# A decoder step with 32 experts: adding the experts' rows to the tokens through DRAM, or on chip with 0/1 matrices

## What is computed

```python
h = h + hier_moe(rmsnorm(h, norm2_g), rg_w, rg_b, re_w, re_b, e_wg, e_wu, e_wd)
...
for gi in range(N_GROUPS):            # 4 groups of 8 experts
    h = silu(einsum('nd,edf->nef', xt, e_wg[gi])) * einsum('nd,edf->nef', xt, e_wu[gi])
    out = out + einsum('nef,efd->nd', h * comb[:, gi, :, None], e_wd[gi])
...
y_prompt, y_sample = rmsnorm(hp, final_g), rmsnorm(hs, final_g)
```

## Time and profile before

| | us |
|---|---|
| median of three runs | 1273.19 (1273.01 to 1273.73) |
| profiled execution | 1273.13 |
| its span | 1271.0 |
| outside its span | 2.1 |

### The profile page before, as it was taken

The page is one execution under the profiler, slowest core; times in us unless marked ns, Lnnn a source line. Parts: engine busy times, 40 slices in busy tenths (PEclk is TensorE's granted clock), DMA queues, the critical chain, the costliest instruction groups (busy, mean ns, idle before and its releaser), DMA issues.

```text
span 1271.0 us, 22247 instructions
## 1 busy us (share of the span) xinstructions
PE 1176.8 (93%) x9742; PEld 851.4 (67%) x9742; DVE 452.2 (36%) x814; ACT 322.7 (25%) x568; POOL 93.1 (7%) x132
## 2 busy tenths in 40 slices
PE   8999899999999999999999998999888887888885
PEld 7889789898898789999998884333333332333331
DVE  5347856553464453333334142121111111111116
ACT  5454333444315452322323231000000000000004
POOL 2100000001000100000000002111111111111100
PEclk9999999999999999999999999999999999999998
DMA  8210103202324822232236488999999999999995
GB/s 244 68 34 2 35 14 82 82 2 72 133 67 127 248 84 76 82 93 75 77 115 223 163 314 318 419 419 417 419 419 420 419 420 419 420 419 419 420 419 215
DMA packets 113419, 283.18 MB, mean 223 GB/s; under 512 B 23779, under 2 KB 71093, under 8 KB 88746
## 3 DMA queue, kind: packets, MB, share of 16 engines
q1 hardware_dynamic: 107546, 269.93, 56.0%
q0 software_dynamic: 5120, 9.46, 2.0%
q10 hardware_dynamic: 656, 2.36, 0.5%
HBM read 273.44 MB, written 15.60 MB: 227 GB/s over the span
## 4 chain that ended last, share of the span: by engine, by line
PE 66%; DMA 19%; DVE 6%; SPq 6%; issue 1%; ACT 1%; DVEq 0%; ACTq 0%
DMA slot<-in_e_wu_dram 18%; PE bank L1465 7%; PE bank L670 7%; PE bank L1398 6%; PE bank L1400 6%; PE bank L1399 6%; SPq L619 6%; PE bank L677 4%; PE bank L1525 2%; PE bank L1526 2%; PE bank L1527 2%; PE bank L1684 1%; PE bank L1638 1%; PE bank L1695 1%; PE bank L1577 1%
## 5 line engine op out<-in xcount | busy, mean ns | idle before, releaser
L670 PE MATMUL bank<-slot,xs 128*64 128x512 f32 x512 | 248.3, 634 | 60.8 <-DMA slot<-in_e_wu_dram 59.9
L671 PE MATMUL bank<-slot,xs 128*64 128x512 f32 x512 | 249.4, 637 | 0.0
L670 PEld LDWEIGHTS bank<-slot,xs 128*64 128x64 f32 x512 | 69.8, 145 | 204.5 <-issue 201.4
L1034 DVE TENSOR_TENSOR xs<-bank,g2x 128x512 f32<-128x512 f32 x32 | 22.1, 691 | 315.6 <-PE bank L803 315.6
L1398 PE MATMUL bank<-xnh,wh 128*128 128x256 f32 (+1 forms) x448 | 133.1, 297 | 0.6 <-DVE mt L3029 0.6
L1400 PE MATMUL bank<-xnh,low 128*128 128x256 f32 (+1 forms) x448 | 132.6, 296 | 0.0
L1399 PE MATMUL bank<-xnl,wh 128*128 128x256 f32 (+1 forms) x448 | 132.6, 296 | 0.0
L905 ACT ACTIVATE sg<-bank 64x512 f32<-64x512 f32 x32 | 19.0, 593 | 444.2 <-PE bank L671 444.2
L2581 DVE TENSOR_TENSOR low<-ring,wh 128x1536 fp32r<-128x1536 f32 (+1 forms) x45 | 89.9, 2005 | 78.2 <-ACT wh L2220 71.1
L677 PE MATMUL bank<-slot,ht 128*64 128x512 f32 x512 | 116.9, 598 | 0.5 <-DVE ht L1062 0.5
L1398 PEld LDWEIGHTS bank<-xnh,wh 128*128 128x128 f32 x448 | 85.0, 190 | 1.3 <-issue 1.2
(11 more groups left out here) (529 smaller groups left out, 2096.5 us busy)
## 6 DMA issues: line engine op xcount, KB each, us to landing
slot<-in_e_wg_dram SPq DMA_DIRECT2D x64, 1024.0 KB, 27.7
slot<-in_e_wu_dram SPq DMA_DIRECT2D x64, 1024.0 KB, 27.8
slot<-in_e_wd_dram SPq DMA_DIRECT2D x64, 1024.0 KB, 28.2
ring<-in_w_in_dram SPq DMA_DIRECT2D x13, 1024.0 KB, 5.4
ring<-in_w_in_dram SPq DMA_DIRECT2D x24, 512.0 KB, 4.3
ring<-in_w_branch_dram SPq DMA_DIRECT2D x24, 256.0 KB, 4.8
kvs<-in_cache_mem_k_dram SPq DMA_DIRECT2D x8, 512.0 KB, 5.7
kvs<-in_cache_mem_v_dram SPq DMA_DIRECT2D x8, 512.0 KB, 5.9
```

The costliest lines, as they stand in the source:

```text
L670: pe.matmul(out[64:128, :], tok, wg[:, FF * k:FF * k + FF], start=(k == 0), stop=(k == KD - 1))
L671: mm = pe.matmul(out[0:64, :], tok, wu[:, FF * k:FF * k + FF], start=(k == 0), stop=(k == KD - 1))
```

## The change

- The scatters, the list of their rows, the clearing of two experts' rows and the reading back are removed. POOL only gathers.
- A token's slot and expert are one number, its code (slot times 32 plus expert). TensorE copies the codes of all tokens to all partitions (`code12` against the identity; ACT to `vsel`). `pcode` holds the code that each partition of a pair's stacked block stands for. DVE's `choose(i)` compares them: `wse[c]`, 128 slots of experts 2i and 2i + 1 by 576 tokens, is 1 where the token chose that slot.
- Routing weights by slot and expert (`cs`) come from 20 further small products. ACT scales an expert's output by them on the way from PSUM (`yh`, rounded for a fast matmul), DVE forms what the rounding left (`yl`). `flip` puts an odd expert's halves the other way round, so that two experts' outputs stack to 128 partitions.
- `mix(i, t)`: four matmuls add the stacked block to token tile t in two PSUM banks (`yh` by two column halves, then `yl`). DVE's `add` brings the sum into `h`. A pair's five tiles stand inside the next odd expert's `gate_up`, one behind each of steps 2 to 6; the last pair's follow the last `down`.
- Gate/up and down have one PSUM bank each instead of two. DVE makes `h2` before `evacuate(e + 1)`, and `yl` before `ht`.
- SP's load of expert 2's third matrix waits for the slot weights (`pe_t` "weights") instead of `wcol`.

The core of the diff (helpers, the overflow loops and tile lists are left out):

```diff
@@ moe_sp
-            dve_t.wait(sp, "weights")
+            pe_t.wait(sp, "weights")
...
-            for n in range(2):
-                sp.wait_ge(scattered[n], 16 * (EX // 2 - 1))
-            sp.wait_ge(cleared, 32)
             general_sp(sp)
-            for t, (t0, tn) in enumerate(TILES):
-                for k in range(2):
-                    sp.dma_start(yb[t][0:tn, D * k:D * k + D], y_d.rearrange("(n k) d -> n k d", k=2)[t0:t0 + tn, k, :])\
-                        .then_inc(yb_loaded[t][k], 16)
@@ moe_pe
-            dve_t.wait(pe, "weights")
+            dve_t.wait(pe, "lists")
             for i in range(2):
                 for t, (_, tn) in enumerate(TILES):
                     to = psum[6 - 2 * i][:, 128 * t:128 * t + tn] if t < 4 else psum[5][:, 64 * i:64 * i + 64]
-                    for p in (0, 64):
-                        mm = pe.matmul(to[p:p + 64, :], wcol[0:tn, 5 * i + t, :], ident[0:tn, 0:tn], start=True, stop=True)
+                    mm = pe.matmul(to, code12[0:tn, i, t:t + 1].to_broadcast([tn, 128]), ident[0:tn, 0:tn], start=True, stop=True)
+            pe_t.done(mm, "codes")
+            idle_products(pe, 7, 8)
+            dve_t.wait(pe, "cw")
+            cw = post[:, :, :, :].rearrange("p k t e -> p (k t) e")
+            for n in range(10):
+                tn = TILES[n % 5][1]
+                for p in (0, 64):
+                    mm = pe.matmul(psum[HT_BANK][p:p + 64, 0:EX], place1[0:tn, n, :], cw[0:tn, n, :], start=(n == 0), stop=(n == 9))
             pe_t.done(mm, "weights")
-            idle_products(pe, 7, 8)
+            def mix(i, t):
+                t0, tn = TILES[t]
+                n = 5 * i + t
+                if t == 0:
+                    dve_e.wait(pe, ("chosen", i))
+                    act_e.wait(pe, ("yh", 2 * i + 1))
+                if n >= 2:
+                    pe.wait_ge(added, n - 1)
+                for y in (yh, yl):
+                    if t == 0 and y is yl:
+                        dve_e.wait(pe, ("yl", 2 * i + 1))
+                    for c in range(2):
+                        mm = pe.matmul(psum[MIX_BANK[n % 2] + c][0:tn, :], wse[c][:, t0:t0 + tn], y[:, c, :],
+                                       start=(y is yh), stop=(y is yl))
+                mm.then_inc(mixed, 1)
             def gate_up(e):
...
+                for k in range(KD):
...
+                    mm = expert_in(pe, psum[0], xs[e % 2], slots[3 * e % NSLOT], slots[(3 * e + 1) % NSLOT], range(k, k + 1))
...
+                    if e >= 3 and e % 2 and 2 <= k <= 6:
+                        mix(e // 2 - 1, k - 2)
             def down(e):
                 dve_e.wait(pe, ("ht", e))
-                if e >= 2:
-                    dve_e.wait(pe, ("y", e - 2))
+                if e >= 1:
+                    dve_e.wait(pe, ("yl", e - 1))
+                    act_e.wait(pe, ("yh", e - 1))
...
+            down(EX - 1)
+            for t in range(5):
+                mix(TWO - 1, t)
             general_pe(pe)
@@ moe_act
+            for e in range(EX + 1):
+                if e < EX:
...
+                    act_e.done(act.activation(sg[:, :], psum[0][64:128, :], ACT.Silu), ("silu", e))
...
+                if e:
+                    pe_m.wait(act, ("d", e - 1))
+                    if e % 2 and e >= 3:
+                        act.wait_ge(mixed, 5 * (e // 2))
+                    for r in range(2):
+                        rows_ = slice(64 * r, 64 * r + 64)
+                        last = act.activation(yh[rows_, r ^ (e - 1) % 2, :], psum[Y_BANK][rows_, :], ACT.Copy, scale=cs[rows_, e - 1:e])
+                    act_e.done(last, ("yh", e - 1))
@@ moe_dve
+            def choose(i):
+                if i >= 1:
+                    dve.wait_ge(mixed, 5 * i)
+                for c in range(2):
+                    last = dve.tensor_scalar(wse[c][:, :], vsel[:, 0, :], pcode[:, c, i:i + 1], None, ALU.is_equal)
+                seq(last)
+                for c in range(2):
+                    last = dve.scalar_tensor_tensor(wse[c][:, :], vsel[:, 1, :], pcode[:, c, i:i + 1], wse[c][:, :], ALU.is_equal, ALU.add)
+                dve_e.done(last, ("chosen", i))
+            def add(i, t):
...
+                dve.wait_ge(mixed, n + 1)
+                hv = h[0:tn, t, :].rearrange("p (c n) -> p c n", c=2)
+                dve.tensor_tensor(hv, hv, banks8[0:tn, bank:bank + 2, :], ALU.add).then_inc(added, 1)
             evacuate(0)
+            act_t.wait(dve, "codes")
             for e in range(EX + 1):
-                if e + 1 < EX:
-                    evacuate(e + 1)
+                if e >= 3 and e % 2:
+                    for t in range(5):
+                        add(e // 2 - 1, t)
...
+                if e + 1 < EX:
+                    evacuate(e + 1)
                 if e:
-                    pe_m.wait(dve, ("d", e - 1))
-                    if e >= 3:
-                        dve.wait_ge(scattered[(e - 1) % 2], 16 * ((e - 1) // 2))
-                    dve_e.done(dve.tensor_copy(yo[(e - 1) % 2][:, :], psum[4 + (e - 1) % 2][:, :]), ("y", e - 1))
+                    act_e.wait(dve, ("yh", e - 1))
+                    for r in range(2):
...
+                        last = dve.scalar_tensor_tensor(yl[rows_, c, :], psum[Y_BANK][rows_, :], cs[rows_, e - 1:e], yh[rows_, c, :],
+                                                        ALU.mult, ALU.subtract)
+                    dve_e.done(last, ("yl", e - 1))
...
+                if e % 2:
+                    choose(e // 2)
...
+            for t in range(5):
+                add(TWO - 1, t)
             general_dve(dve)
...
+            for t in range(5):
+                final(t)
@@ moe_pool
-            gather(0)
-            for e in (EX - 2, EX - 1):
-                pool.indirect_dma_start(y_rows, bass.IndirectOffsetOnAxis(il[:, 1, e:e + 1].bitcast(U32), 0), xg[1][:, :], None,
-                                        bounds_check=4 * NT - 1, oob_is_err=False).then_inc(cleared, 16)
-            pool.wait_ge(cleared, 32)
-            for e in (1, 2):
+            for e in range(EX):
                 gather(e)
-            for e in range(EX - 2):
-                if e + 3 < EX:
-                    gather(e + 3)
-                dve_e.wait(pool, ("y", e))
-                pool.indirect_dma_start(y_rows, bass.IndirectOffsetOnAxis(il[:, 1, e:e + 1].bitcast(U32), 0), yo[e % 2][:, :], None,
-                                        bounds_check=4 * NT - 1, oob_is_err=False).then_inc(scattered[e % 2], 16)
```

More of the change, by code:

```diff
@@ L591, in build @@
         dve_o = Steps(sem("dve_o"), ["wr"] + [x for c in range(OUTS) for x in [("h", c, t) for t in range(5)] + ([("lg", c)] if c < OUTS - 1 else [])])
[L592 to L597, removed]
+        pe_t = Steps(sem("pe_t"), ["pos", "lists", "codes", "weights"])
+        mixed, added = sem("mixed"), sem("added")
+        TWO = EX // 2
+        act_t = Steps(sem("act_t"), ["root"] + [("x2", t) for t in range(5)] + ["exp_g", "exp_e", "codes"])
+        dve_t = Steps(sem("dve_t"), ["clear", "sumsq", "ms", "rstd", "lg", "dg", "sel", "places", "rows", "code", "lists", "addr", "de", "c12", "cw"])
+        dve_l = Steps(sem("dve_l"), ["zeros", "even", "gather0", "scatter0", "gather", "scatter"] + [("more", t, k) for t in range(5) for k in range(2)])
         pool_t = Steps(sem("pool_t"), ["far", "rows", "xg"])
@@ L806, in gate_up @@
             def gate_up(e):
                 dve_e.wait(pe, ("xs", e))
-                if e >= 2:
[L809 to L814, removed]
+                if e >= 1:
+                    dve_e.wait(pe, ("h", e - 1))
@@ L895, in moe_act @@
             act_t.done(act.activation(pg[:, 3, :], pg[:, 3, :], ACT.Exp), "exp_e")
-            pe_t.wait(act, "weights")
+            pe_t.wait(act, "codes")
             for i in range(2):
-                act.activation(wsel[:, i, 0:SEQ], psum[6 - 2 * i][:, :], ACT.Copy)
-            act_t.done(act.activation(wsel[:, :, SEQ:NT], psum[5][:, 0:2 * NS].rearrange("p (i n) -> p i n", i=2), ACT.Copy), "weights")
-            for e in range(EX):
-                pe_m.wait(act, ("gu", e))
-                if e >= 1:
-                    dve_e.wait(act, ("h", e - 1))
-                act_e.done(act.activation(sg[:, :], psum[e % 2][64:128, :], ACT.Silu), ("silu", e))
@@ L1181, in general_act @@
         def general_act(act):
-            dve_e.wait(act, ("h", EX - 1))
             with act.If(some_overflow(act)):
@@ L1212, in general_dve @@
                         dve_n.done(dve.tensor_copy(yg[:, :], psum[4][:, :]), "y")
+                dve.wait_ge(yb_loaded, 16 * 5)
+                for t, (_, tn) in enumerate(TILES):
+                    for k in range(2):
+                        if k:
+                            dve_l.wait(dve, ("more", t, 0))
+                        dve_l.done(dve.scalar_tensor_tensor(h[0:tn, t, :], yb[t][0:tn, D * k:D * k + D], c12[0:tn, k, t:t + 1], h[0:tn, t, :],
```

(4 more changed lines are left out.)

213 lines of the change are left out of this document (88 added, 125 removed).

## The result

The changed kernel took 1277.3 us (median of 20 runs, 1274.5 to 1283.2), the one before 1273.8 us in the same session (20 runs, 1270.7 to 1276.7): a ratio of 1.0032 (95% interval 1.0023 to 1.0040), so slower by a third of a per cent. The profiled execution took 1277.25 us, its span is 1275.5. The time forecast was 1275.1.

The account below looks back on a forecast made before the run. Transfers bound the loop before; TensorE was to become the bound. Loop end at 1242.7 plus 30.3 behind it gives a span of 1273.0, with 2.1 outside 1275.1 us against 1273.13; range 1260 to 1288.

Parts of the forecast that it names:

- The likeliest case: Over the loop: TensorE becomes the bound at the prices of the rows, 1275.1 us, within 1270 to 1280; chance 0.60.
- The switches: Mixed tiles in `gate_up`: 0.91 us streaming plus 0.09, 0.10, 0.09 and 0.05 for array changes, 1.25 a tile, 6.25 a pair.
- The hidden loads of the rival: At the switches in mixed tiles, loads go ahead of the matmuls: a tile costs 1.10 us, 1264 us in all; chance 0.13.
- The loop's end: Last gate and up products at 1242.7 us, 7.8 later than before: 791.64 + 0.3 + 357.0 + 93.8.
- Beside TensorE: ACT's and DVE's scaling and adds (1.25 us each) in the loop hide behind TensorE, which waits for none of them.
- the rival of the late low part: In `gate_up`, mixing waits for `yl`: 1297 us; chance 0.20, shared with other TensorE waits of 0.5 to 1.2 us a pair.
- The end: From the last gate and up products to the span's end: 30.3 us instead of 36.1, so 5.8 us won.
- the double evacuation: Behind each of the last two `down`s: `yh` 1.2 us, then `yl` 1.25 and 1.3; one copy of 0.69 stood there before.
- One sign: Late in the expert loop, the DMA engines' busy share was to fall below 1.

Follow-up runs that it names:

- Fewer stops: The changed kernel with a pair's five tiles mixed at three places of the gate instead of five: 1267.46 us, ratio 0.9944.
- the doubled low part: The changed kernel with the two matmuls of the low part issued twice in every tile: 1315.57 us, ratio 1.0316.
- the kernel with fewer bytes: The changed kernel with the third matrix loaded for experts 0 to 2 only and used for all others: 1277.24 us, ratio 1.0029.
- The kernel that mixes beside the transposes: The changed kernel with tiles two behind step 4, two right ahead of `turn_in`, one right behind it: 1264.35 us, the second time 1265.39 us.
- the last experiment: The kernel mixing beside the transposes, with the last `down` in another PSUM bank and the last `ht` ahead of `yl`: 1259.58 us, ratio 0.9878.

## Why the prediction was right

The likeliest case came true: TensorE became the bound and took back what the lighter transfers allowed. The time came out 2.2 us above the forecast, inside its range. The forecast time, 1.9 us above the kernel before, would have counted as no change; the 3.5 us measured are slower by more than 0.2%, which its range held too.

- **The switches.** A pair cost 6.29 us ((1244.05 - 792.65 - 357.0) / 15) where 6.25 were forecast from rows of other products. Fewer stops (0.33 us for a way in and back) and the doubled low part (0.47 a tile for two matmuls) measure the two shares apart: 0.92 + 0.34 = 1.26, where 1.25 was forecast. The Trainium skill, "TensorEngine Tiling (Array Packing)", section "Key Properties", states that a change of the tiling mode drains TensorE. The trace agrees, with 0.1 us at each change. The other part of the price is a load that isn't hidden. The hidden loads of the rival, 11 us less, are seen at no switch here.
- **The loop's end.** It was forecast for 1242.7 and came at 1244.05: 0.7 from a later start, 0.6 from the pairs. The first `turn_in` came 1.40 us later than before (773.15 against 771.75), where 0.9 was forecast, and the way from there to the `turn_in` behind the second expert was 0.39 us shorter, where 0.6 was. Both executions lost 1.7 us on that way to a lower clock (below). The forecast had no term for it, and that it cancels is luck. The 0.5 us of the first `turn_in` can't be put down to the codes: in the eight profiles with the new routing it comes anywhere from 771.73 to 774.42.
- **Beside TensorE.** This step held: the adds take 1.22 us (1.25 forecast), and TensorE waits for none of them in the loop; the 0.6 us in the table above lie behind the last `down`. The low part comes in time, but with less room than I had counted. `yl` is done 2.4 us after `gate_up` starts (2.0 forecast) and wanted 0.9 later; the rival of the late low part was that far off.
- **The end** was the term furthest off: 31.45 us, not 30.3. Most of it is the double evacuation, forecast from the Silu and the copy of a similar shape. ACT's two blocks take 1.38 us, not 1.2, and DVE's 1.51, not 1.25, and each stands twice on the path: 0.44 the first time and 0.39 the second. With the hand-over between engines the first add starts 14.6 us behind the last gate and up products instead of 13.5, and the steps behind it took what was forecast.
- **One sign was wrong.** I wrote that the DMA share would fall below 1 late in the loop. It stayed at 1.01 until 1225 us. With 30.1 us of TensorE to 30.7 of transfers a pair the DMA engines always had loads in hand, though fewer of them, as the landing of a load shows (in the median 15 to 17 us after its issue instead of 28), and they ended 16 us before the loop did. By these two numbers alone the transfers would be the slower side; it is the store of three experts' weights at the start that kept TensorE from ever waiting for them. What showed that they weren't the bound were TensorE's idle time and the kernel with fewer bytes, not their share.

## What to carry to other kernels

Moving work from a full resource to one with slack is worth only what that slack leaves, and the slack is to be counted over the whole loop. Where transfers set the pace TensorE had 3.8 us an expert to spare, and mixing takes only 3.1. But the loop begins on weights in store: from its start to the last gate and up products TensorE's chain had 86.3 us to spare before (1234.90 - 791.64 - 357.0; 59.9 us of it waits for weights, beside them a clock of 0.95 from 880 us on the earlier trace rows), and the mixing, which streams for 69 us, took 94.4 by ten changes of the array's shape a pair. Count what small products cost with the ways in and back, and put products of one shape together, best beside such as are there already: the same matmuls at other places made 13 us. When a change turns a single evacuation into two that follow each other, look at the last item, where nothing hides them.

## What the runs showed of the hardware that was not expected

**The clock falls behind short pauses, in some executions.** The kernel that mixes beside the transposes was profiled twice. In both, TensorE stands idle for 2.86 us ahead of the last `down`. Windows over that pause and the `down`, first of one execution:

```profile
1237.00:1238.90 1.90, 0.00 (x1) 0.00 (x1) 1.82 (x4) 0.00 (x0) 0.00 (x0) 1.00 0.00 0
1238.90:1242.50 3.60, 3.60 (x16) 1.06 (x16) 2.47 (x4) 0.00 (x0) 0.00 (x0) 1.00 0.00 0
```

then of the other:

```profile
1235.00:1236.80 1.80, 0.00 (x0) 0.00 (x0) 1.75 (x3) 0.00 (x0) 0.00 (x0) 1.00 0.00 0
1236.80:1240.50 3.70, 3.65 (x12) 1.24 (x14) 2.50 (x4) 0.00 (x0) 0.00 (x0) 0.64 0.00 0
```

In the second the granted clock falls to the lower of its two levels (1.2 instead of 2.4 GHz) for most of the `down` behind the pause, which takes 5.35 us instead of 3.65. Seven profiled executions have this pause, of 2.86 to 2.88 us. In five of them the last `down` takes 5.30 to 6.64 us, in two (the changed kernel and the first one here) 3.65. At the start of the loop there is such a place too, behind the routing's small products and their gaps. Windows over the first `gate_up` of the changed kernel:

```profile
774.00:775.30 1.30, 0.54 (x4) 0.24 (x6) 0.69 (x1) 0.00 (x0) 0.63 (x1) 0.97 0.57 139
775.30:778.60 3.30, 3.30 (x10) 0.91 (x8) 0.00 (x0) 0.00 (x0) 0.37 (x1) 0.50 0.99 412
```

From the first `turn_in` to the second it took 10.32 us there, and 8.62 in the second execution above, with the clock at 1.00. Of the seven executions, the two that have no fall behind the late pause are the two that have this one. The kernel before has such a stretch in its second `gate_up`:

```profile
780.00:800.00 20.00, 18.63 (x82) 7.04 (x82) 4.01 (x7) 1.19 (x2) 3.04 (x3) 0.91 1.01 421
```

From its second `turn_in` to the third lie 11.44 us, and 9.76 without the scatters, with the clock at 1.00 there. The spread of the runs fits their mean granted clocks: of the 20 runs of the changed kernel the 15 with 0.988 or more took up to 1278.6 us, the four with 0.987 1279.4 to 1280.3, and the one with 0.983 1283.2. In the profile of the last experiment, where the pause is gone, the last `down` runs at a clock of 1.00. That filling a pause always keeps the clock up isn't shown by one execution.

**A scaled copy isn't a Silu.** Of one shape, 64 by 512 from PSUM, ACT takes 0.683 us for the copy that scales by partition and rounds for the fast matmul, and 0.595 for the Silu. The groups of the changed kernel from 880 to 1220 us:

```profile
L1061 DVE SCALAR_TENSOR_TENSOR yl<-bank,cs,yh 64x512 fp32r<-64x512 f32 x45 | 33.7, 750 | 87.0 <-ACT yh L899 86.7
L899 ACT ACTIVATE yh<-bank,cs 64x512 fp32r<-64x512 f32 x46 | 31.4, 683 | 84.7 <-PE bank L668 84.4
...
L1053 DVE TENSOR_TENSOR h<-sg,bank 64x512 f32<-64x512 f32 x23 | 15.6, 678 | 30.7 <-ACT sg L889 27.6 <-PE bank L800 3.0
L1013 DVE TENSOR_TENSOR xs<-bank,g2x 128x512 f32<-128x512 f32 x23 | 15.5, 675 | 0.0
...
L889 ACT ACTIVATE sg<-bank 64x512 f32<-64x512 f32 x23 | 13.7, 595 | 219.5 <-PE bank L662 219.5
```

On DVE, half the partitions are no cheaper: a product of two tensors takes 0.678 us for 64 by 512 (`h2`) and 0.675 for 128 by 512 (`xs`). The form for `yl`, which also scales, takes 0.750 for 64 by 512.
